# Asking for the query and branch weights whole, behind the last sum of the other half, in a hybrid conv/retention block on 8 cores

## The reference

```python
xm = rmsnorm(x, norm_w) * (1.0 + sc_x) + sh_x          # adaLN, sc/sh from silu(c) @ ada_w
h, bg, cg, za, q, k, v, zb, ga, gb = split(xm @ w_in)   # 1024 x 9216 weights
ret = bidir_retention(rope(q), rope(k), v, ...)         # 8 heads, both directions, chunks of 128
conv_out = dwconv_centred(cg * h, conv_w, conv_b)
y_a = (silu(za) * bg * conv_out) @ w_a
y_b = (silu(zb) * groupnorm(ret)) @ w_b
y = (sigmoid(ga) * y_a + sigmoid(gb) * y_b) @ w_out
out = rmsnorm(x + g_x * y, final_norm_w)
```

## Time and profile before

| | |
|---|---|
| median of three timed runs | 1021.64 us (896.77 to 1036.5) |
| profiled execution | 893.57 us |
| span of its slowest core, 0 | 892.0 us |
| spans of all cores | 887.2 to 892.0 us |
| PE busy | 798.3 us, 89% of the span |
| DVE / ACT / POOL busy | 454.6 / 360.7 / 321.7 us |
| TensorE's granted clock | mean 0.985 on core 0; 1.00 in every stretch of 20 us from 100 to 240 us |
| DMA, queue of the hardware kind (SP's) | 60.44 MB, 26.5% of 16 engines |
| DMA, queue of the software kind (POOL's) | 27.27 MB, 18.6% of 16 engines |

### The profile page before, as it was taken

One profiled execution on the slowest core, in us unless ns is written; L12 is line 12 of the kernel. 1 busy time (PEld: TensorE's weight loads), 2 busy tenths in 40 slices (PEclk: granted clock), 3 DMA queues, 4 the chain that ended last, 5 costly groups with the idle time before them and its releaser, 6 DMA issues.

```text
span 892.0 us, 14050 instructions; the slowest of 8 cores (887.2 to 892.0 us)
## 1 busy us (share of the span) xinstructions
PE 798.3 (89%) x4399; PEld 385.5 (43%) x4480; DVE 454.6 (51%) x1058; ACT 360.7 (40%) x641; POOL 321.7 (36%) x344
## 2 busy tenths in 40 slices
PE   0179999989876998998989999999999999999996
PEld 0145445444443444444444444444444444444443
DVE  3458525889575766657524423443365511344336
ACT  3489656787455443443431221222122211122122
POOL 0136425666565444444410213212242233232333
PEclk9999999999897999999999999999999999999999
DMA  8997906999391222214440543345006070035133
GB/s 244 284 287 173 176 19 119 190 214 148 61 158 28 42 40 42 43 38 63 83 84 12 104 86 48 58 85 95 1 1 141 9 181 1 13 108 163 69 121 142
DMA packets 75999, 88.61 MB, mean 99 GB/s; under 512 B 54923, under 2 KB 61195, under 8 KB 74518
## 3 DMA queue, kind: packets, MB, share of 16 engines
q1 hardware_dynamic: 70022, 60.44, 26.5%
q0 software_dynamic: 5904, 27.27, 18.6%
HBM read 93.72 MB, written 8.39 MB: 114 GB/s over the span
## 4 chain that ended last, share of the span: by engine, by line
PE 75%; DMA 6%; DVE 5%; ACT 5%; issue 3%; POOL 2%; SPq 1%; DVEq 0%; POOLq 0%; ACTq 0%
PE P L1020 52%; PE P L583 12%; PE P L1284 6%; DMA kz<-x 6%; ACT tm L998 2%; DVE vb L1035 2%; PE P L701 2%; DVE cm L972 1%; ACT st L923 1%; SPq L478 1%; PE P L643 1%; PE P L964 1%; DVE tm L570 1%; PE P L965 1%; DMA vb<-tm 0%
## 5 line engine op out<-in xcount | busy, mean ns | idle before, releaser
L1020 PE MATMUL P<-xmt,vb 128*128 128x512 bf16 x1254 | 281.2, 379 | 4.0 <-DVE wt L1183 1.8
L1020 PEld LDWEIGHTS P<-xmt,vb 128*128 128x128 bf16 x1280 | 124.5, 98 | 152.6 <-issue 3.6
L583 PE MATMUL P<-wt,xmt 128*128 128x512 bf16 x667 | 160.2, 389 | 9.0 <-ACT xmt L504 4.8
L1020 PE MATMUL P<-xmt,wt 128*128 128x512 bf16 x494 | 115.9, 384 | 2.9 <-ACT tm L998 1.9
L1186 POOL TENSOR_TENSOR kz<-tm,wt 128x1024 bf16<-128x1024 f32 x16 | 45.7, 2856 | 161.3 <-DVE wt L1183 161.3
L583 PEld LDWEIGHTS P<-wt,xmt 128*128 128x128 bf16 x688 | 65.9, 100 | 85.5 <-issue 15.9
L1020 PEld LDWEIGHTS P<-xmt,wt 128*128 128x128 bf16 x512 | 50.0, 99 | 59.9 <-issue 5.4
L1263 DVE SCALAR_TENSOR_TENSOR tm<-tm,P 128x512 f32<-128x512 f32 x32 | 22.0, 688 | 87.2 <-PE P L1020 87.2
L1139 DVE TENSOR_TENSOR wt<-P,wt 128x512 f32<-128x512 f32 x32 | 22.1, 692 | 81.4 <-ACT wt L1138 60.0
L1020 PE MATMUL P<-vb,wt 128*128 128x512 bf16 x256 | 58.9, 381 | 5.3 <-DVE vb L1035 5.3
L1265 POOL TENSOR_TENSOR st<-st,tm 128x512 bf16<-128x512 bf16 x32 | 39.8, 1244 | 65.4 <-DVE tm L1263 65.4
(11 more groups left out here) (170 smaller groups left out, 1097.4 us busy)
## 6 DMA issues: line engine op xcount, KB each, us to landing
kz<-x SPq DMA_DIRECT2D x24, 512.0 KB, 7.2
wt<-x SPq DMA_DIRECT2D x24, 512.0 KB, 4.6
vb<-w_conv POOLq DMA_DIRECT2D x16, 512.0 KB, 9.3
out<-wt SPq DMA_DIRECT2D x15, 512.0 KB, 2.7
st<-ada_w SPq DMA_DIRECT2D x2, 2048.0 KB, 14.0
wt<-ada_w SPq DMA_DIRECT2D x2, 2048.0 KB, 28.9
vb<-w_mix POOLq DMA_DIRECT2D x8, 512.0 KB, 11.1
cm<-rope SPq DMA_DIRECT2D x33, 64.0 KB, 3.2
```

Source lines behind the costliest of these rows:

```text
L583: ins = e.matmul(pf(bank)[:, 0:wid], lhsT=lhs_x(ch, k), rhs=w[:, k, c0_:c0_ + wid], start=(k == 0), stop=(k == 7))
L1020: ins = e.matmul(pf(bank), lhsT=lhs(k), rhs=rhs(k), start=(k == 0), stop=(k == 7))
```

## The change

The six parts leave the loop over own pairs, and both weight matrices are requested whole with `wload` right behind the last sum of the other half. No arithmetic changes, and nothing else moves.

```diff
@@ -678,6 +678,8 @@
             if p == 0:
                 P.op("dve", lambda e: e.tensor_copy(out=xmTh, in_=xm[0][:, :, 0:2]), reads=["xm0_0"], writes=["xmTh"])
         g_acc(other[7], range(4), 4, False, True)
+        wload("wq", wq, wq_d)
+        wload("wzb", wzb, wzb_d)
 
         def f_ksum(e):
             ins = None
@@ -850,14 +852,6 @@
                 load2(9 + p + 3)
             rope2(9 + p + 2)
             sq2(9 + p + 2)
-            if p in (1, 2):
-                k0 = 4 * (p - 1)
-                P.dma("pool", lambda e, k0=k0: e.dma_start(out=wq[:, k0:k0 + 4, :], in_=wq_d[:, k0 * 512:(k0 + 4) * 512].rearrange("p (k c) -> p k c", k=4)),
-                      f"wq{k0}", writes=[f"wq{k0}"])
-            if p in (3, 4, 5, 6):
-                k0 = 2 * (p - 3)
-                P.dma("pool", lambda e, k0=k0: e.dma_start(out=wzb[:, k0:k0 + 2, :], in_=wzb_d[:, k0 * 1024:(k0 + 2) * 1024].rearrange("p (k c) -> p k c", k=2)),
-                      f"wzb{k0}", writes=[f"wzb{k0}"])
             w1(hi)
             if prev:
                 w2(prev)
```

## The result

The changed kernel is slower: median 932.65 us of four runs (923.17 to 948.91) against 959.2 of four (896.66, 896.77, 1021.64 and 1036.5) before. Some executions of both kernels were disturbed (1021.64 and 1036.5 before, 948.91 after), and the ratio leaves those out: **1.0366, 95% interval 1.0209 to 1.0522**. The forecast was 889.5 us. The profiled execution took 923.17 us, and its slowest core is now core 1.

The account below looks back on a forecast made before the run. TensorE's beat was taken to bound the own stage. Core 0's 892.0 us less 4.2 (2.5 issues, 1.7 traffic) gives 887.8; 0.2 for three cores meeting and 1.57 around the span make 889.5 us, range 885.5 to 895.5.

Parts of the forecast that it names:

- The beat and the excess: Own stage: TensorE's fourteen halves need 78.8 us; core 0 takes 83.3, and each core loses at least 2.8 us.
- Six issues leave the stage: Own stage, pairs 2 to 5: without POOL's issue ahead of L806, L497 ends 0.63 us earlier; gain 2.5 us per core.
- proof of blocking: Own stage: L497 loses all 1.61 us of its overlap with POOL, so the full 0.63 us a pair is gained.
- The weight traffic leaves the stage: Own stage: transposes and x loads are no longer late beside weight parts; gain 1.7 us on cores 0 and 3.
- Two issues ahead of the memset: POOL before the memset of gT: two issues cost 1.2 us, covered by 4.6 us of slack; cost 0.
- Their traffic comes in at 103 to 126 us: cost 0: Ahead of the own stage: 3072 KB of weights land near 126 us, at worst 132, delaying nothing; cost 0.
- Next in line, a rigid shift: After the own stage: TensorE is on its beat, the stage's end moves up on all cores, and nothing after it moves.
- C: Rival, ahead of the own stage: POOL stands behind the two large transfers, 8.4 us slower, 902 us; chance 0.04.
- A: Rival, own stage: only the traffic matters; core 0 gains 1.7 us, core 5 nothing, time 891.9 us; chance 0.12.
- B: Rival, own stage: nothing moves, L497 stays late by L806 and DMA lateness comes from the transposes; 893.6 us, chance 0.11.
- something on another core that I don't see: Remaining chance of 0.05 for an effect on another core, with no place or size named.

Follow-up runs that it names:

- e4: Kernel before with all six weight parts kept in the own stage, each issued behind w1(hi) instead of ahead of it; ratio 1.0011 [0.9975, 1.0048].
- e3: Kernel before with only wq moved whole to the new place, wzb's four parts left in the loop; median 899.85 us, ratio 1.0066.
- e5: Changed kernel with both whole loads behind the memset, which waits for the transposes of pair 0; 890.0 us, ratio 0.9932 against the kernel before.
- e9: Changed kernel with the transposes of own pair 0 requested only after both weights have landed; 894.14 us, ratio 0.9998 against the kernel before.
- e2: Changed kernel with the same 3072 KB at the same place in six parts of 512 KB; profiled 894.28 us, ratio 1.0013 against the kernel before.
- e7: Changed kernel with wzb cut by columns into two loads of 1024 KB, beside whole wq; profiled execution 896.45 us.

## Why the prediction was wrong, point by point

*The beat and the excess* were right: fifteen L823 in 79.12 to 79.15 us on five cores and up to 79.74 on the others (two of them, 79.27 and 79.28, inside the 78.8 to 79.3 that I gave, core 5 not).

*Six issues leave the stage* was right in its size and only half right in its reason. Core 0 of the changed kernel, timeline of pair 3, which answers to the earlier trace rows:

```profile
184.51 1.04 POOL L808 TENSOR_TENSOR tm<-tm,cm 128x512 bf16<-128x512 bf16 x1
...
185.51 1.05 POOL L809 TENSOR_TENSOR tm<-tm,cm 128x512 bf16<-128x512 bf16 x1
185.57 2.56 DVE L497 TENSOR_SCALAR xmt<-xmt,cm 128x256 bf16<-128x256 bf16 x4
186.69 1.10 POOL L790 CAST st<-tm 64x1024 bf16<-64x1024 f32 x1
...
188.39 5.34 PE L583 MATMUL P<-wt,xmt 128*128 128x512 bf16 x23
```

L497 is 2.56 us long instead of 3.19, the 0.63 forecast, and ends 1.57 us after L809 as before (1.58). L583 has no wait. With 2.5 us forecast, core 7 gained 2.29, core 5 1.81 and core 1 2.45, and the undisturbed cores of e4 came to 2.8 under core 7 with the issue behind the decays. The whole 0.63 came, not half.

But the prediction's proof of blocking was none: that L497 "loses 3.19 - 1.58 = 1.61, all of it" takes the 1.58 from the same three times as the 1.61, so the two must be equal. And 1.58 is not what L497 needs when nothing holds it: four of them took 1.25 us on core 1 of the changed kernel at 164.26. Core 7 before, POOL behind L807, and the third of the four L497 of the earlier trace rows:

```profile
180.81 1.11 POOL L788 CAST st<-tm 64x1024 bf16<-64x1024 f32 x1
```

```profile
L497 DVE TENSOR_SCALAR xmt<-xmt,cm x1: 1057/1057/1057, 180.9 to 180.9; 128x256 bf16<-128x256 bf16 x1
```

The first L497, 1.704 us long, ends 0.09 us after L807; the third, 1.057 long, ends with L788, the copy of the state. The two others take 0.33 each. So L497 is held twice, by the decays and by the copy, and the issue mattered because it moved all three. (The Trainium skill, page SBUF — State Buffer, section Who interferes with whom, calls the shared port pair an exclusive lock; by that rule the term is the full 0.63, and these rows agree.)

*The weight traffic leaves the stage* was right for its sizes: with the term before, 4.16 us on core 0 against 4.2 and 4.04 on core 3 against 4.1. Core 2, whose stage I had not read, gained 3.61. Its picture was too kind: I took the 1.7 us for a property of cores 0 and 3. e3 and e4 show that it is a collision that strikes any core, by 0 to 7.7 us.

*Two issues ahead of the memset* was right: issued at 103.0 and 103.6 on core 1, the memset at 104.10, and DVE L695 waits, as before, for ACT and not for the memset.

*Their traffic comes in at 103 to 126 us: cost 0.* This step failed. The cost was 36.3 us on core 1 and 6.4 to 30.6 on the others, by which the first sum came later. It has three faults. First, I named the transposes for pair 0 as being on the road with the weights and then gave a due date only to the x loads (135.61). The transposes have one as well: L504 starts on them at 128.54 on core 1 before, 27 us after the issue of the later one. I had a cover of 27 us in hand and did not write it down. Second, I priced the company by rows without it: 21.8 us was scaled from wgb and wb, which have no transpose beside them, and for the other side I tripled the x load of 10.67. The 21.8 was good for weights alone (23.3 in e5, 25.6 in e9, and 29.1 as the upper bound holds). In company it was 30.8 to 60.1. Third, the x loads missed their own date: they took 29.5 to 54.3 us and landed between 135 (core 0) and 167 (core 1). That is hidden behind the transposes on most cores, but on cores 2, 5 and 6 ACT waits for them as well. Core 2 of the changed kernel:

```profile
153.84 1.06 ACT L451 ACTIVATE wt<-kz 128x1024 bf16<-128x1024 f32 x1 [3.77 <-DMA kz<-x]
```

The row that should have warned me was the earlier trace rows: ACT waited 2.12 us for a *transpose* beside one part of 512 KB. I had read it as a matter of 1.7 us in the stage and had not asked what the same meeting would cost with loads two and four times larger and with no beat of several pairs to absorb it.

*Next in line, a rigid shift* was right. From the first sum to the end, less the stage, cores need 656 to 663 us in all kernels here; what is lost or won ahead of it reaches the end unchanged.

*The rivals.* C forecast 902 by the mechanism that POOL stands behind the two loads. Its side was right and its mechanism was not: POOL issued both in 1.1 us and went on. The loads held up the DMA engines, and by them ACT. A and B, both inside the range, are refuted by e4, whose cores 0, 2 and 3 lose nothing in the stage with all the traffic still in it. I gave 0.05 to "something on another core that I don't see"; it was on all of them, in a step that I had written.

## What to carry to other kernels

List every transfer that is in flight when a new one comes in, and write beside each who reads it and when; a transfer priced at nothing needs a due date and a price from a row in the same company. Take care above all with a DMA transpose on a short leash beside a large load: here either order, loads behind the transposes (e5) or transposes behind the loads (e9), starts the own stage at most 8.3 us later than before (e5 0.7 or less, e9 3.4 to 8.3), and both at once up to 36.3. When a load is moved because it is in the way, make it wait for the transfer that it would meet: that is e5, the only kernel here that ran clearly under the one before. To move its issue past one instruction (e4) freed TensorE on three cores but did not bring the time down, since the loads still met transposes in the stage. And when the profile shows one engine's instruction held by another engine, look at each instruction of the group by itself before naming the holder.

## What the hardware showed that I had not expected

A DMA transpose and a large load slow each other far beyond their bytes. The DMA records of core 1 of e9, 131 to 133 us, with the two transposes of pair 0 and nothing else:

```profile
DMA packets 1593, 0.40 MB, mean 200 GB/s; under 512 B 1593, under 2 KB 1593, under 8 KB 1593
...
q1 hardware_dynamic: 1593, 0.40, 104.8%
```

And of core 1 of the changed kernel, 140 to 150 us, while ACT waits for the same transposes:

```profile
DMA packets 390, 0.60 MB, mean 60 GB/s; under 512 B 353, under 2 KB 353, under 8 KB 353
...
q1 hardware_dynamic: 346, 0.09, 99.9%
q0 software_dynamic: 44, 0.52, 25.2%
```

A packet of SP's queue takes 1.048 x 2 us x 16 / 1593 = 0.021 us alone and 0.999 x 10 x 16 / 346 = 0.46 us here, some twenty times as long. The engines are busy by the record and move 60 GB/s instead of 200. For each packet of a weight (11.8 KB) about eight small ones get through. Nor is it bandwidth, by the records, that the transposes wait for at the end. The same core, 155 to 163 us, when they have yet to land:

```profile
DMA packets 12, 0.10 MB, mean 12 GB/s; under 512 B 6, under 2 KB 6, under 8 KB 6
```

(The Trainium skill, page DMA: Bandwidth & Descriptors, section Queues, rings and completion order, says that a DMA engine alternates between its queues packet by packet. By that rule a small packet would at times stand behind a large one, and finer cut loads would hurt less; e2 and e7 against the change agree in direction. It explains neither the eight to one nor the stretch with 12 packets. The same page, section Rules for kernel authors, says that a transpose next to ordinary DMAs needs nothing; the row is about transposes that corrupt each other's data. For the speed, the runs here show a need: 61.8 us against 6.7.)

What stays open is why the packets of the two disturb each other by so much more than the bytes: 3072 KB in 60 us is less than half the rate at which they come in without transposes (25.6 for wzb, e9). Whether it is the transposes' writing, the cast on the way or the turn-taking between the queues was not separated. The x loads, which have no cast, land in 3.6 to 6.0 us right behind the transposes in the kernel before, but they are in the same queue; a large load without a cast beside transposes would be the next experiment, and it wasn't tried.
